# Expert rows and gated products turned by VectorE's 32x32 block transpose, in a two-layer trunk on one Trainium2 core

## What is computed

```
def expert_block(args):
    xe, e = args
    return (jax.nn.silu(xe @ w_gate[e]) * (xe @ w_up[e])) @ w_down[e]
h = modulate(rms_norm(x, norm2_g[layer]), sh2, sc2)
x = x + g2[:, None, :] * moe_ffn(h, w_router, b_router, w_gate, w_up, w_down)
```

## Time and profile before

| | us |
|---|---|
| median of 3 runs (lowest to highest) | 2285.79 (2285.34 to 2285.99) |
| the profiled execution's own time | 2287.5 |
| span of its trace | 2285.7 |
| PE busy in the span | 2058.2 (90%) |
| VectorE busy | 1167.0 (51%) |
| ScalarE busy | 661.4 (29%) |
| POOL busy | 325.8 (14%) |
| mean granted TensorE clock | 0.950 |

### The profile page before, as it was taken

One profiled execution on the slowest core, in us unless ns is written; L12 is line 12 of the kernel. 1 busy time (PEld: TensorE's weight loads), 2 busy tenths in 40 slices (PEclk: granted clock), 3 DMA queues, 4 the chain that ended last, 5 costly groups with the idle time before them and its releaser, 6 DMA issues.

```text
span 2285.7 us, 51476 instructions
## 1 busy us (share of the span) xinstructions
PE 2058.2 (90%) x19986; PEld 1133.8 (50%) x19987; DVE 1167.0 (51%) x2325; ACT 661.4 (29%) x1629; POOL 325.8 (14%) x601
## 2 busy tenths in 40 slices
PE   6999999999999489999999399998993899999991
PEld 3444444556666345555555266654442455555550
DVE  3555400678997622322222579999865222222225
ACT  4111101567776322222222310003351122222222
POOL 0010100000000122222222300010001122222223
PEclk9999999899999799999999599999996999999996
DMA  9466501003300846658686403241043977824746
GB/s 395 153 237 251 178 26 37 1 19 148 148 10 10 308 167 246 223 199 317 255 310 254 177 1 98 83 124 47 0 177 141 375 291 257 312 71 153 262 151 230
DMA packets 117717, 391.04 MB, mean 171 GB/s; under 512 B 22848, under 2 KB 43968, under 8 KB 112256
## 3 DMA queue, kind: packets, MB, share of 16 engines
q1 hardware_dynamic: 67968, 302.95, 35.0%
q0 software_dynamic: 21632, 67.76, 8.4%
q10 hardware_dynamic: 28032, 19.17, 2.8%
HBM read 337.56 MB, written 47.49 MB: 168 GB/s over the span
## 4 chain that ended last, share of the span: by engine, by line
PE 76%; DVE 14%; DMA 5%; issue 2%; ACT 2%; SPq 1%; POOL 0%; ACTq 0%; DVEq 0%; POOLq 0%
PE ps L1536 22%; PE ps L1550 11%; PE ps L1374 10%; DVE kv L1256 9%; PE ps L1681 5%; PE ps L1427 5%; PE ps L1483 5%; PE ps L1441 3%; PE ps L1454 3%; PE ps L1466 3%; PE ps L1528 2%; PE ps L1543 2%; DMA ring<-in_w_gate_up 1%; DMA kv<-in_w_ada 1%; PE ps L1609 1%
## 5 line engine op out<-in xcount | busy, mean ns | idle before, releaser
L1152 DVE TENSOR_TENSOR hT<-hT,ps 128x128 f32<-128x128 f32 x146 | 42.1, 288 | 515.8 <-ACT hT L726 515.8
L1536 PE MATMUL ps<-kv,hT 128*32 128x256 f32 x4800 | 275.9, 382 | 9.9 <-DMA kv<-in_w_gate_up 6.3
L1536 PE MATMUL ps<-ring,hT 128*32 128x256 f32 x4544 | 265.6, 386 | 17.9 <-issue 10.6
L1256 DVE SCALAR_TENSOR_TENSOR kv<-kv,cols 128x640 f32<-128x640 f32 (+1 forms) x330 | 266.2, 807 | 11.2
L726 ACT ACTIVATE hT<-ps 128x128 f32<-128x128 f32 x146 | 40.4, 277 | 709.1 <-PE ps L1536 709.1
L1609 PE MATMUL ps<-hT,ring 128*128 128x320 f32 (+1 forms) x768 | 225.4, 454 | 6.3 <-ACT hT L611 6.3
L1374 PE MATMUL ps<-hT,ring 128*128 128x512 f32 x512 | 222.4, 592 | 1.6 <-ACT hT L611 1.6
L1536 PEld LDWEIGHTS ps<-kv,hT 128*32 128x32 f32 x4800 | 155.1, 110 | 104.7 <-issue 13.7
L1536 PEld LDWEIGHTS ps<-ring,hT 128*32 128x32 f32 x4544 | 150.3, 111 | 109.2 <-issue 24.7
L989 DVE TENSOR_TENSOR_SCAN pbuf<-hT 128x128 f32<-128x128 f32 (+7 forms) x128 | 173.3, 1354 | 48.3 <-ACT hT L662 48.1
L719 ACT ACTIVATE hT<-ps,modc 128x32 f32<-128x32 f32 x592 | 175.1, 376 | 68.2 <-PE ps L1528 68.2
(11 more groups left out here) (251 smaller groups left out, 2378.8 us busy)
## 6 DMA issues: line engine op xcount, KB each, us to landing
ring<-in_w_gate_up SPq DMA_DIRECT2D x128, 512.0 KB
kv<-in_w_gate_up SPq DMA_DIRECT2D x128, 512.0 KB
kv<-in_w_ada SPq DMA_DIRECT2D x21, 2048.0 KB, 8.3
ring<-in_w_down SPq DMA_DIRECT2D x64, 512.0 KB
kv<-in_w_down SPq DMA_DIRECT2D x64, 512.0 KB
expert_rows<-hT ACTq DMA_DIRECT2D x584, 32.0 KB
ring<-in_w_in SPq DMA_DIRECT2D x8, 2048.0 KB, 9.3
expert_rows<-ring POOLq DMA_DIRECT2D x2, 7680.0 KB, 23.6
```

Source lines behind the costliest of these rows:

```text
L1256: ins = V.scalar_tensor_tensor(new, old, w_dw_c[:, c, k:k + 1], new, ALU.mult, ALU.add)
L1536: ins = mm(bank(0)[UNIT * q:UNIT * (q + 1), 0:2 * P], xT[:, c, :], wset[s][q // 2][:, 512 * c + 256 * (q % 2):512 * c + 256 * (q % 2) + 25 ...
```

## The change

`xs`, in place of POOL's copy, becomes the 32x32 block transpose of `xg[u]` by VectorE: partition 32q + k, column 32c + t then holds row t's channel 256q + 32c + k. So chunk c of `xs` is 32 rows by the 128 channels {256q + 32c + k}, and the rows of the gate and up weights are laid out in this channel order on the host. Likewise `haT` is the block transpose of `ha`, and the rows of `w_down` follow. Scale and shift now differ by partition and chunk: two `tensor_tensor` with a broadcast operand (128x256) take the place of eight small instructions, from columns in the new order (`modc` 4 and 5, loaded by 16 more small DMAs on POOL's queue, and 2 more `make_modc`). ACT has no `keep` left, PE no `turn_rows` and no `turn_ha`, POOL no copy of rows. `gate_up` now waits for `ha_made` itself (bank 0 is read by `gated_half`).

```diff
+        def mod_quarter(l, j, q):
+            at = (6 * l + j) * D + QUARTER * q
+            return mod_dram[at:at + QUARTER].rearrange("(c r) -> r c", r=UNIT)
...
+                    for k, j in enumerate((shift, scale)):
+                        if n >= 4:
+                            for q in range(QUARTERS):
+                                pool.dma_start(modc[UNIT * q:UNIT * (q + 1), n, k, :],
+                                               mod_quarter(l, j, q)).then_inc(modc_loaded, 16)
...
-            for n in range(1, 4):
+            for n in range(1, 6):
                 load_modc(n)
...
                 with pool.Fori(0, pairs) as i:
-                    for u in (1, 0):
-                        n = 2 * i + 2 - u
-                        pool.wait_ge(x_gathered[l][u], 16 * i + 32 - 16 * u)
-                        pool.wait_ge(x_turned2[l], n)
-                        nc.gpsimd.tensor_copy(idx_now[:, u:u + 1], slot_tok[:, ds(n + 2, 1)])
-                        nc.gpsimd.tensor_copy(xs, xg[u]).then_inc(x_ready[l], 1)
+                    for u in range(2):
+                        pool.wait_ge(x_turned[l], 2 * i + u + 1)
+                        nc.gpsimd.tensor_copy(idx_now[:, u:u + 1],
+                                              slot_tok[:, ds(2 * i + u + 2, 1)]).then_inc(idx_next[l], 1)
...
                     for u in range(2):
                         silu(2 * i + u)
-                        keep(2 * i + u + 1)
                         store(2 * i + u - 1, 1 - u)
...
+                moved, scaled = (modc[:, 4 + l, k, :].unsqueeze(2).to_broadcast([P, DC, UNIT]) for k in range(2))
+
+                def scale_rows(b, u, gathers, first=False):
+                    dve.wait_ge(x_gathered[l][u], 16 * gathers)
+                    if not first:
+                        dve.wait_ge(xT_kept[l], b)
+                    V.transpose(xs, xg[u]).then_inc(x_turned[l], 1)
+                    dve.wait_ge(x_turned[l], b + 1)
+                    V.tensor_tensor(xs_c, xs_c, scaled, ALU.mult).then_inc(x_scaled[l], 1)
+
+                def move_rows(b):
+                    dve.wait_ge(x_scaled[l], b + 1)
+                    V.tensor_tensor(xT, xs_c, moved, ALU.add).then_inc(xT_kept[l], 1)
...
-                def keep_ha(b):
-                    dve.wait_ge(ha_turned[l], b + 1)
-                    V.tensor_copy(haT, bank(2)[:, 0:P]).then_inc(haT_kept[l], 1)
+                def turn_ha(b):
+                    dve.wait_ge(ha_made[l], b + 1)
+                    V.transpose(haT, ha).then_inc(haT_kept[l], 1)
...
                 with dve.Fori(0, pairs - 2) as j:
                     for u in range(2):
+                        dve.wait_ge(up_done[l], 2 * j + u + 5)
+                        move_rows(2 * j + u + 5)
+                        dve.wait_ge(haT_kept[l], 2 * j + u + 4)
                         gated_half(2 * j + u + 4)
-                        keep(2 * j + u + 5)
                         dve.wait_ge(y_stored[l][1 - u], 16 * QUARTERS * j + 16 * QUARTERS * (u + 1))
                         keep_y(2 * j + u + 3, 1 - u)
-                        keep_ha(2 * j + u + 4)
+                        turn_ha(2 * j + u + 4)
+                        scale_rows(2 * j + u + 6, u, j + 4)
...
-                def gate_up(b, s):
+                def gate_up(b, s, first_unit=False):
                     pe.wait_ge(xT_kept[l], b + 1)
-                    pe.wait_ge(xT_kept2[l], b + 1)
+                    if not first_unit:
+                        pe.wait_ge(ha_made[l], b)
...
                     with pe.Fori(first + 1, end) as b:
                         gate_up(b, s)
-                        pe.wait_ge(x_ready[l], b + 1)
-                        turn_rows()
                         pe.wait_ge(w_loaded[s][2], 16 * PARTS * (E // 2 * l + 1) + 16 * PARTS * i)
                         down(b - 1, s)
-                        turn_ha(b)
```

More of the change, by code:

```diff
@@ L713, in moe @@
                 keep_scores(l, 1)
-                def keep(b):
-                    act.wait_ge(x_turned[l], b + 1)
-                    for q in range(QUARTERS):
-                        c = 2 * q
-                        ins = nc.scalar.activation(xT[:, c, :], bank(4)[:, UNIT * q:UNIT * (q + 1)],
-                                                   ACT.Identity, bias=modc[:, 2 * l + 1, 0, c:c + 1],
-                                                   scale=modc[:, 2 * l + 1, 1, c:c + 1])
-                    ins.then_inc(xT_kept[l], 1)
                 def silu(b):
@@ L1011, in _ @@
                 if p == DC:
-                    dve.wait_ge(modc_loaded, 32 * 3)
-                    for n in range(1, 4):
+                    dve.wait_ge(modc_loaded, 32 * (2 * QUARTERS + 3))
+                    for n in range(1, 6):
                         make_modc(n)
@@ L1161, in keep_y @@
                                     bcC[:, 0:QUARTER], ALU.mult).then_inc(y_kept[l], 1)
-                keep(0)
+                dve.wait_ge(modc_made, 6)
+                scale_rows(0, 0, 1, first=True)
+                move_rows(0)
+                scale_rows(1, 1, 1)
                 dve.wait_ge(gate_loaded, 80 * (l + 1))
                 pairs = dve.value_load(bounds[0:1, E + 1:E + 2], min_val=MINBLK * E // 2, max_val=MAXBLK // 2)
-                gated_half(0)
-                keep(1)
-                keep_ha(0)
-                for b in (1, 2, 3):
+                for b in range(4):
+                    dve.wait_ge(up_done[l], b + 1)
+                    move_rows(b + 1)
+                    if b:
+                        dve.wait_ge(haT_kept[l], b)
                     gated_half(b)
-                    keep(b + 1)
                     if b == 3:
                         dve.wait_ge(y_stored[l][0], 16 * QUARTERS)
-                    keep_y(b - 1, (b - 1) % 2)
-                    keep_ha(b)
+                    if b:
+                        keep_y(b - 1, (b - 1) % 2)
+                    turn_ha(b)
+                    scale_rows(b + 2, b % 2, b // 2 + 2)
                 with dve.Fori(0, pairs - 2) as j:
                     for u in range(2):
+                        dve.wait_ge(up_done[l], 2 * j + u + 5)
+                        move_rows(2 * j + u + 5)
+                        dve.wait_ge(haT_kept[l], 2 * j + u + 4)
                         gated_half(2 * j + u + 4)
-                        keep(2 * j + u + 5)
                         dve.wait_ge(y_stored[l][1 - u], 16 * QUARTERS * j + 16 * QUARTERS * (u + 1))
                         keep_y(2 * j + u + 3, 1 - u)
-                        keep_ha(2 * j + u + 4)
+                        turn_ha(2 * j + u + 4)
+                        scale_rows(2 * j + u + 6, u, j + 4)
                 before = dve.value_load(bounds[0:1, E + 2:E + 3], min_val=MINBLK * E // 2 - 1, max_val=MAXBLK // 2)
@@ L1539, in gate_up @@
                     ins.then_inc(up_done[l], 1)
-                def turn_ha(b):
-                    pe.wait_ge(ha_made[l], b + 1)
-                    nc.tensor.transpose(bank(2)[:, 0:P], ha, ident[:, :]).then_inc(ha_turned[l], 1)
                 def down(b, s):
@@ L1755, in col, with quarter_col @@
         return v.reshape(-1, P).T
+    def quarter_col(v):
+        return v.reshape(QUARTERS, DC, UNIT).transpose(0, 2, 1).reshape(P, DC)
     def rows(w, k):
@@ L1761, in gate_up @@
     def gate_up(gate, up):
-        halves = [v.reshape(-1, DC, P, 2, 2, P) for v in (gate, up)]
+        halves = [v.reshape(-1, QUARTERS, DC, UNIT, 2, 2, P).transpose(0, 2, 1, 3, 4, 5, 6).reshape(-1, DC, P, 2, 2, P)
+                  for v in (gate, up)]
         w = np.stack(halves, axis=5).transpose(0, 3, 2, 1, 4, 5, 6)
@@ L1785 @@
         "w_gate_up": gate_up(a["moe_w_gate"], a["moe_w_up"]),
-        "w_down": rows(a["moe_w_down"], F // P),
+        "w_down": rows(a["moe_w_down"].reshape(-1, QUARTERS, F // P, UNIT, D).transpose(0, 2, 1, 3, 4), F // P),
         "w_taps": shifts.transpose(1, 4, 2, 3, 0).reshape(P, P),
```

69 lines of the change are left out of this document (22 added, 47 removed).

## The result

The changed kernel takes 2181.02 us (median; 2176.75 to 2181.59) against 2285.89 (2285.34 to 2287.55), a ratio of 0.9538 (95% interval 0.9524 to 0.9552): 104.9 us less. The prediction had 85.3 less and a range that ended at 2190. So the sign held, and TensorE was the bound as forecast, but more came back than the sum allowed. An experiment given with one time was executed once: its whole time has no interval, and what it tells is read from the hand-overs in its trace (the time from one `gate_up`'s start to the next). The profiled execution took 2181.59 (span 2179.4, clock 0.94), 106.3 less than the span before.

What follows compares the result with a forecast made beforehand. The prediction took TensorE to bound the expert units; 72.1 us from regular hand-overs, 9.6 from expert changes, 3.4 and 0.6 from layer starts and ends, less 0.4, made 85.3 off 2285.8: 2200 us, range 2190 to 2235.

Steps and rivals of the forecast that it cites:

- the sum: Whole kernel: 72.1 us from regular unit hand-overs, 9.6 expert changes, 3.4 and 0.6 layer starts and ends, less 0.4: 85.3 us.

## What to carry to other kernels

Take an engine's rate from steps inside an unbroken stream of one form, never from a stretch that ends in another form, and price a removed instruction as the step across it less the step without it. On TensorE, full-width instructions among matmuls on 32-column tiles are dear for the change of width, not for what they move: take them off, or make them in the width of their neighbours (0.22 against 0.40 to 0.51). When units get shorter, look at what the sequencer does between them: register loads placed in the middle of a unit cost nothing here, behind a loop end they cost 0.7 and 1.3 us.

## What the runs showed of the hardware that I had not expected

- A full-width pair of instructions between 32-column streams costs 0.45 us with one moving column each and 0.51 with 128; one full-width transposition costs 0.40; eight 32-column records of 128 columns cost 0.22. The weight loads at a full-width seam start with their matmuls and not ahead of them.
- VectorE's block transposes in float32 take 0.30 us (128x128) and 0.40 (128x256); back to back they start 0.20 and 0.33 apart.
- Behind waits of 3.7 to 4.3 us for weights TensorE's granted clock is 0.56 to 0.60 in the mean of the next 6 us, so that a `gate_up` of 3.66 takes 6.0 to 6.2; behind waits of 1.7 and 2.8 us it stayed at 1.00.
- TensorE's sequencer needs 1.96 us from the end of an inner loop over two loads of a bound to the next unit's start, 2.6 with an outer loop's end between; none of it shows when the loads stand in mid unit.
- A wait that stands in TensorE's order holds its sequencer even when the engine has work left: with the product's transposition behind `down` the sequencer leaves the loop 0.05 us behind the product's end, without it 0.45 behind `down`'s start, and at a change of expert that difference of 0.5 us is paid in full.
